# Encoder trunk: the first four weight units opened together, x loaded in four pieces and turned in a triangle

## Chip, cores and metric

One core of a Trainium2 chip. The metric is device microseconds of one execution; the kernel before takes 1910.95 us, the median of 3 runs (1910.9 to 1911.2).

## What is computed

A two-layer encoder trunk in float32 on 512 tokens (two sequences of 256) of width 1024, with shared weights. Both layers are a feed-forward half step, a mixer and a second feed-forward half step, each behind an RMS norm:

```python
def rmsnorm(x, g):
    y = xf * lax.rsqrt(jnp.mean(xf * xf, axis=-1, keepdims=True) + EPS)
    return (y * g.astype(jnp.float32)).astype(x.dtype)

def swiglu(x, wg, wu, wd):
    return (jax.nn.silu(x @ wg) * (x @ wu)) @ wd

for layer in range(DEPTH):
    x = x + 0.5 * swiglu(rmsnorm(x, norm_g[layer, 0]), ...)
    x = x + mix            # pooling and Hyena convolution, then neighbourhood attention
    x = x + 0.5 * swiglu(rmsnorm(x, norm_g[layer, 2]), ...)
```

The feed-forward width is 2816. The change touches only the start: the load of x and the first columns of the first feed-forward.

## The kernel before

Activations lie transposed: eight chunks of 128 channels by 512 tokens. A **unit** is 128 output columns of a weight matrix, 8 (or 11) tiles of 128x128. SyncE loads it (512 KB) into one of four buffers raw0 to raw3 (L255), ScalarE makes the high part wh (L288), VectorE the low part wl (L295), and TensorE multiplies three times for each chunk k, wh by xh, wh by xl and wl by xh (L832, L835, L836, one **triple**). There are two buffers wh and two wl, used by turns. A unit of 8 chunks is 24 products into one PSUM bank.

The phase `up0` takes 11 rounds of four units (gate, up, gate, up; j = 0 to 3). Units are counted through: round 0 has units 0 to 3, round 1 has units 4 to 7. VectorE scales each bank by the norm factor rbc (L610), ScalarE takes Silu of the gate (L349), VectorE multiplies (L620) and splits into hh (L353, ScalarE) and hl (L622). The split of unit u is written into each engine's program behind the end of unit u-2 (`ahead`, `split_high`), and SyncE loads unit u when the low split of unit u-3 is done.

The norm's factor is not needed by the products, since it is applied behind them. ScalarE squares each chunk (L337), GpSimd sums them (L1152), TensorE takes the mean by a product with a constant matrix (`norm_mean`, L885), ScalarE takes the root (L341), and VectorE the reciprocal (`norm_factor`, L597).

The opening before the change: ScalarE's queue issues the constants `cst` (the identity among them) and the parameter rows `vrow`; SyncE's queue loads x in four transfers and then weights. TensorE turns vrow (L889), then all of x in 32 transposes into the eight banks (L897). VectorE copies each bank to x (L662), ScalarE makes xh (L335) and its square (L337), VectorE xl (L584). Two weight units are split among these. TensorE goes through unit 0 chunk by chunk, waiting for each xl. Behind its eighth square ScalarE issues seven transfers that lay out a bias table in memory (L397, `bias_by_column<-in_rpb`), which the attention reads much later. In `first` the mean stands behind the first triple of unit 1, and reciprocal and scaling run beside units 1 and 2.

Each engine works its own program in order. A semaphore wait holds all that stands behind it on that engine.

## Time and profile before

| | |
|---|---|
| median of 3 runs | 1910.95 us |
| span of the profiled execution | 1909.3 us |
| around the span (median less span) | 1.65 us |
| TensorE busy | 1887.2 us, 99% |
| VectorE busy | 921.8 us, 48% |
| ScalarE busy | 647.1 us, 34% |
| GpSimd busy | 79.7 us, 4% |

The profiled execution's own time is not listed apart from its span; 1.65 us is what lies between the span and the median of the runs. Busy time of TensorE counts pipelined products, so its share says that it hardly pauses and not that it is at its peak. Names of the form ACTq are a queue's DMA issues, which the engine's busy time does not contain.

### The profile page before, as it was taken

How to read it: one execution, taken by the hardware profiler on the slowest of the kernel's cores; microseconds unless marked ns; L12 is line 12 of the kernel's file. 1: busy time of each engine (PE TensorE's matmuls, PEld its weight loads, DVE VectorE, ACT ScalarE, POOL GpSimd, SP SyncE). 2: the span in 40 equal slices, each digit the busy share in tenths (PEclk: the TensorE clock that was granted, in tenths of full speed). 3: DMA queues.
4: the chain of work that ended last, by engine and by line, in shares of the span. 5: the costliest groups of instructions: out<-in, count | busy, mean ns of one | idle time of the engine just before them, and what ended most of it. 6: DMA issues, size and time to landing. Idle time of an engine off the chain costs nothing.

```text
span 1909.3 us, 23383 instructions
## 1 busy us (share of the span) xinstructions
PE 1887.2 (99%) x8579; PEld 1537.3 (81%) x8579; DVE 921.8 (48%) x1166; ACT 647.1 (34%) x859; POOL 79.7 (4%) x63
## 2 busy tenths in 40 slices
PE   6999999999999999999999999999999999999999
PEld 5888888878688888888888888888777788888887
DVE  6444444366555444433544443336776654444321
ACT  4333332233243333322333232225656533333221
POOL 2000000012300000000000000001111000000000
PEclk9999999999999999999999999999999999999999
DMA  6333333243033333333233334323222133333331
GB/s 174 92 98 99 99 105 101 81 133 92 30 91 97 99 97 91 113 97 97 78 99 99 97 91 120 91 83 94 64 82 83 55 100 93 94 99 103 112 107 52
DMA packets 349165, 180.34 MB, mean 94 GB/s; under 512 B 12922, under 2 KB 347525, under 8 KB 349126
## 3 DMA queue, kind: packets, MB, share of 16 engines
q1 hardware_dynamic: 333504, 169.89, 30.6%
q10 hardware_dynamic: 15622, 9.93, 2.0%
q8 instruction: 24, 0.39, 0.1%
q14 instruction: 15, 0.12, 0.0%
HBM read 177.70 MB, written 3.93 MB: 95 GB/s over the span
## 4 chain that ended last, share of the span: by engine, by line
PE 98%; DVE 1%; DMA 0%; ACT 0%; issue 0%; ACTq 0%
PE bank L832 31%; PE bank L836 30%; PE bank L835 30%; PE bank L957 1%; PE bank L1138 1%; PE bank L1122 1%; PE bank L970 1%; PE bank L948 1%; DVE xl L584 0%; DMA vrow<-in_v_params 0%; PE bank L978 0%; PE bank L1110 0%; PE bank L937 0%; PE bank L885 0%; PE bank L1088 0%; PE bank L922 0%
## 5 line engine op out<-in xcount | busy, mean ns | idle before, releaser
L295 DVE TENSOR_TENSOR wl<-raw,wh 128x1024 fp32r<-128x1024 f32 (+1 forms) x296 | 393.4, 1329 | 685.5 <-ACT wh L288 684.1
L832 PE MATMUL bank<-xh,wh 128*128 128x512 f32 x1728 | 682.6, 395 | 6.7 <-DVE xl L584 6.7
L835 PE MATMUL bank<-xl,wh 128*128 128x512 f32 x1728 | 674.0, 390 | 0.0
L836 PE MATMUL bank<-xh,wl 128*128 128x512 f32 x1728 | 673.5, 390 | 0.0
L288 ACT ACTIVATE wh<-raw 128x1024 fp32r<-128x1024 f32 (+1 forms) x296 | 333.7, 1127 | 515.4 <-PE bank L836 515.0
L832 PEld LDWEIGHTS bank<-xh,wh 128*128 128x128 f32 x1728 | 324.8, 188 | 85.9 <-issue 12.9
L836 PEld LDWEIGHTS bank<-xh,wl 128*128 128x128 f32 x1728 | 325.0, 188 | 68.6
L835 PEld LDWEIGHTS bank<-xl,wh 128*128 128x128 f32 x1728 | 325.1, 188 | 66.4 <-issue 1.4
L832 PE MATMUL bank<-hh,wh 128*128 128x512 f32 x704 | 274.9, 391 | 0.0
L836 PE MATMUL bank<-hh,wl 128*128 128x512 f32 x704 | 274.0, 389 | 0.0
L835 PE MATMUL bank<-hl,wh 128*128 128x512 f32 x704 | 273.9, 389 | 0.0
L832 PEld LDWEIGHTS bank<-hh,wh 128*128 128x128 f32 x704 | 132.2, 188 | 28.1 <-issue 1.2
L836 PEld LDWEIGHTS bank<-hh,wl 128*128 128x128 f32 x704 | 132.2, 188 | 27.6
L835 PEld LDWEIGHTS bank<-hl,wh 128*128 128x128 f32 x704 | 132.2, 188 | 27.3
L353 ACT ACTIVATE hh<-ua 128x512 f32 (+1 forms) x88 | 55.6, 632 | 247.3 <-DVE ua L620 247.3
L349 ACT ACTIVATE ga<-ga 128x512 f32<-128x512 f32 x88 | 55.7, 632 | 165.9 <-DVE ga L610 165.9
L622 DVE TENSOR_TENSOR hl<-ua,hh 128x512 f32 (+1 forms) x88 | 61.0, 693 | 79.2 <-ACT hh L353 79.2
L335 ACT ACTIVATE xh<-x,vec 128x512 fp32r<-128x512 f32 (+1 forms) x48 | 34.7, 723 | 132.4 <-DVE x L655 125.2
L610 DVE TENSOR_TENSOR ga<-bank,rbc 128x512 f32<-128x512 f32 x100 | 68.4, 684 | 8.9 <-PE bank L836 8.8
L610 DVE TENSOR_TENSOR ua<-bank,rbc 128x512 f32<-128x512 f32 x88 | 60.2, 684 | 12.1 <-PE bank L836 12.1
L620 DVE TENSOR_TENSOR ua<-ga,ua 128x512 f32<-128x512 f32 x88 | 60.9, 692 | 5.8 <-DVE ua L610 0.5
L584 DVE SCALAR_TENSOR_TENSOR xl<-x,vec,xh 128x512 fp32r<-128x512 f32 (+1 forms) x48 | 40.6, 856 | 37.1 <-ACT xh L335 37.1
(144 smaller groups left out, 1023.4 us busy)
## 6 DMA issues: line engine op xcount, KB each, us to landing
raw<-in_ffn_w_gate SPq DMA_DIRECT2D x88, 512.0 KB, 3.8
raw<-in_ffn_w_up SPq DMA_DIRECT2D x88, 512.0 KB, 3.9
raw<-in_ffn_w_down SPq DMA_DIRECT2D x64, 704.0 KB, 4.5
raw<-in_w_qkv SPq DMA_DIRECT2D x24, 512.0 KB, 3.8
raw<-in_w_in_ab SPq DMA_DIRECT2D x16, 512.0 KB, 3.9
raw<-in_w_out_ab SPq DMA_DIRECT2D x8, 512.0 KB, 3.6
raw<-in_w_o SPq DMA_DIRECT2D x8, 512.0 KB, 3.6
braw<-bias_by_column ACTq DMA_DIRECT2D x16, 192.0 KB, 3.8
```

The costliest lines, as they stand in the source:

```text
L288: act.activation(wh[w][:, 0:ph.kt, :], raw[r][:, 0:ph.kt, :], ACT.Copy).then_inc(high, 1)
L295: dve.tensor_tensor(wl[w][:, 0:ph.kt, :], raw[r][:, 0:ph.kt, :], wh[w][:, 0:ph.kt, :].bitcast(F32), ALU.subtract).then_inc(low, 1)
L335: act.activation(xh[:, bass.ds(d, 1), :], x[:, bass.ds(d, 1), :], ACT.Copy, scale=col(V_NORM + norm * KD + d)).then_inc(xh_done, 1)
L349: act.activation(g[:, :], g[:, :], ACT.Silu).then_inc(silu_done, 1)
L353: act.activation(hh[:, bass.ds(f, 1), :], u[:, :], ACT.Copy).then_inc(hh_done, 1)
L584: dve.scalar_tensor_tensor(out=xl[:, bass.ds(d, 1), :], in0=x[:, bass.ds(d, 1), :], scalar=col(V_NORM + norm * KD + d), in1=xh[:, bass.ds( ...
L610: dve.tensor_tensor(out, src, r, ALU.mult).then_inc(evac, 1)
L620: dve.tensor_tensor(u[:, :], g[:, :], u[:, :], ALU.mult).then_inc(h_done, 1)
L622: dve.tensor_tensor(hl[:, bass.ds(f, 1), :], u[:, :], hh[:, bass.ds(f, 1), :].bitcast(F32), ALU.subtract).then_inc(hl_done, 1)
L832: pe.matmul(out, wh[w][:, k, :], hi[:, at, :], start=start, stop=False)
L835: pe.matmul(out, wh[w][:, k, :], lo[:, at, :], start=False, stop=False)
L836: return pe.matmul(out, wl[w][:, k, :], hi[:, at, :], start=False, stop=stop)
```

## The change

x comes in four pieces of 256 channels. Each is two transfers, and behind each stands one of the first four weight loads, without a wait. The constants' identity part is loaded by itself, ahead of vrow, and the rest behind it (`ident_in`, `const_in`). Units 2 and 3 get wh and wl buffers of their own (`wh_c`, `wh_d`, `wl_c`, `wl_d`), which lie where hh will be written later. x is turned two chunks at a time into banks 4 to 7; ScalarE takes xh and VectorE xl from PSUM, VectorE then copies to x. After each pair of chunks one weight unit is split. The products go through chunks and units in a triangle (`opening`). Round 0 of `up0` is taken out of the general loops of all engines and written out, and the seven bias transfers follow at its end on ScalarE.

```diff
--- before.py
+++ after.py
@@ -153,3 +153,4 @@
         hh, hl = region([("hh", [P, KF, TOK], F32R), ("hl", [P, KF, TOK], F32R)])
-        (xrow,) = region([("xrow", [P, TT, D])])
+        xrow, wh_c, wl_c, wh_d, wl_d = region([("xrow", [P, TT, D]), ("wh_c", [P, KD, P], F32R), ("wl_c", [P, KD, P], F32R),
+                                               ("wh_d", [P, KD, P], F32R), ("wl_d", [P, KD, P], F32R)])
         own = ExitStack()
@@ -183,3 +184,3 @@
             ("rqk", [P, 2, TT, 2]), ("kwide", [P, TT, P])])
-        wh, wl = wh + [wh2], wl + [wl2]
+        wh, wl = wh + [wh2, wh_c, wh_d], wl + [wl2, wl_c, wl_d]
@@ -189,2 +190,3 @@
         raw_in = [sem(f"raw_in{s}") for s in range(4)]
+        ident_in = sem("ident_in")
         const_in, vec_in, filt_in, out_in = sem("const_in"), sem("vec_in"), sem("filt_in"), sem("out_in")
@@ -245,8 +247,2 @@
         def _(sp):
-            for n in range(4):
-                half = slice(n // 2 * (D // 2), (n // 2 + 1) * (D // 2))
-                sp.dma_start(xrow[:, n % 2 * 2:n % 2 * 2 + 2, half],
-                             (a["x_sample"] if n % 2 else a["x_prompt"])[0].rearrange("(t p) c -> p t c", p=P)[:, :, half])\
-                  .then_inc(x_in[n], 16)
             def load(ph, i):
@@ -256,4 +252,14 @@
+            for n in range(4):
+                cols = slice(n * 2 * P, (n + 1) * 2 * P)
+                for s, src in enumerate((a["x_prompt"], a["x_sample"])):
+                    sp.dma_start(xrow[:, 2 * s:2 * s + 2, cols], src[0].rearrange("(t p) c -> p t c", p=P)[:, :, cols])\
+                      .then_inc(x_in[n], 16)
+                sp.dma_start(raw[n][:, 0:KD, :], unit_source(phases[0], 0, n)).then_inc(raw_in[n], 16)
             for ph in phases:
-                if ph.name == "w_in":
+                if ph.name == "up0":
+                    with sp.Fori(1, ph.iters) as i:
+                        load(ph, i)
+                elif ph.name == "w_in":
                     for i in range(ph.iters):
@@ -269,3 +275,9 @@
+        def opens(ph, i):
+            return ph.name == "up0" and isinstance(i, int) and i == 0
         def split_place(ph, i, j):
+            if opens(ph, i) and j > 1:
+                return j + 1, j
             return (j if ph.name == "qkv" or early(ph, i, j) else j % 2), j
@@ -285,4 +297,5 @@
             act.wait_ge(raw_in[r], 16 * (ph.uses0[r] + 1 + i))
-            back = 2 if early(ph, i, j) else 1
-            act.wait_ge(unit_done, ph.unit(i, j) - back + UNIT_CREDIT)
+            if not opens(ph, i):
+                back = 3 if ph.name == "up0" and isinstance(i, int) and i == 1 else 2 if early(ph, i, j) else 1
+                act.wait_ge(unit_done, ph.unit(i, j) - back + UNIT_CREDIT)
             act.activation(wh[w][:, 0:ph.kt, :], raw[r][:, 0:ph.kt, :], ACT.Copy).then_inc(high, 1)
@@ -305,3 +318,5 @@
-            if after_first or ph.name in NORM_OF or ph.name == "w_o":
+            if ph.name == "up0":
+                first = 1
+            elif after_first or ph.name in NORM_OF or ph.name == "w_o":
                 body(0, False)
@@ -320,4 +335,5 @@
-            act.dma_start(cst[:, :], a["c_small"]).then_inc(const_in, 16)
+            act.dma_start(ident, a["c_small"][:, C_ID:C_ID + P]).then_inc(ident_in, 16)
             act.dma_start(vrow[:, :], a["v_params"]).then_inc(vec_in, 16)
+            act.dma_start(cst[:, P:C_ALL], a["c_small"][:, P:C_ALL]).then_inc(const_in, 16)
             act.dma_start(zT[:, :], a["c_z"]).then_inc(filt_in, 16)
@@ -383,11 +399,21 @@
+            act.wait_ge(vec_done, 1)
             for d in range(KD):
-                act.wait_ge(evac, d + 1 + EVAC_CREDIT)
-                if d >= 2:
-                    act.wait_ge(acc_done, d - 1)
-                residual_parts(0, d, d % 2)
-                if d == 1:
-                    split_high(act, phases[0], 0, 0)
-                if d == 4:
-                    split_high(act, phases[0], 0, 1)
+                act.wait_ge(x_mm, d + 1)
+                act.activation(xh[:, d, :], bank[4 + d % 4][:, :], ACT.Copy, scale=col(V_NORM + d)).then_inc(xh_done, 1)
+                if d % 2:
+                    split_high(act, phases[0], 0, d // 2)
+                    for e in (d - 1, d):
+                        act.wait_ge(evac, e + 1 + EVAC_CREDIT)
+                        if e >= 2:
+                            act.wait_ge(acc_done, e - 1)
+                        act.activation(sqtmp[:, e % 2, :], x[:, e, :], ACT.Square).then_inc(sq_done, 1)
+            split_high(act, phases[0], 1, 0)
+            act.wait_ge(const_in, 16)
+            norm_std(0)
+            evacuate(phases[0], 0, 0)
+            split_high(act, phases[0], 1, 1)
+            evacuate(phases[0], 0, 1)
+            evacuate(phases[0], 0, 2)
+            evacuate(phases[0], 0, 3)
@@ -555,3 +581,3 @@
             dve.wait_ge(vec_mm, 1)
-            dve.tensor_copy(vec[:, :], bank[7][:, 0:V_ALL]).then_inc(vec_done, 1)
+            dve.tensor_copy(vec[:, :], bank[0][:, 0:V_ALL]).then_inc(vec_done, 1)
             dve.wait_ge(vec_done, 1)
@@ -659,10 +685,11 @@
-            for d in range(KD):
-                dve.wait_ge(x_mm, d + 1)
-                dve.tensor_copy(x[:, d, :], bank[d][:, :]).then_inc(evac, 1)
-            split_low(dve, phases[0], 0, 0)
-            for d in range(KD):
-                part_low(0, d)
-                if d == 4:
-                    split_low(dve, phases[0], 0, 1)
+            for d in range(0, KD, 2):
+                for e in (d, d + 1):
+                    dve.wait_ge(xh_done, e + 1)
+                    dve.scalar_tensor_tensor(out=xl[:, e, :], in0=bank[4 + e % 4][:, :], scalar=col(V_NORM + e),
+                                             in1=xh[:, e, :].bitcast(F32), op0=ALU.mult, op1=ALU.subtract)\
+                       .then_inc(xl_done, 1)
+                for e in (d, d + 1):
+                    dve.tensor_copy(x[:, e, :], bank[4 + e % 4][:, :]).then_inc(evac, 1)
+                split_low(dve, phases[0], 0, d // 2)
@@ -759,2 +786,11 @@
+            norm_factor(0)
+            evacuate(phases[0], 0, 0)
+            split_low(dve, phases[0], 1, 0)
+            evacuate(phases[0], 0, 1)
+            sums_cleared(0)
+            split_low(dve, phases[0], 1, 1)
+            evacuate(phases[0], 0, 2)
+            evacuate(phases[0], 0, 3)
             for ph in phases:
@@ -886,14 +922,48 @@
-            pe.wait_ge(const_in, 16)
-            pe.wait_ge(vec_in, 16)
-            pe.transpose(bank[7][:, 0:V_ALL], vrow[:, :], cst[0:V_ALL, C_ID:C_ID + V_ALL]).then_inc(vec_mm, 1)
-            for d in range(KD):
-                if d % 4 == 0:
-                    pe.wait_ge(x_in[d // 4 * 2], 16)
-                    pe.wait_ge(x_in[d // 4 * 2 + 1], 16)
-                if d == 7:
-                    pe.wait_ge(vec_done, 1)
-                for t in range(TT):
-                    last = pe.transpose(bank[d][:, t * P:(t + 1) * P], xrow[:, t, d * P:(d + 1) * P], ident)
-                last.then_inc(x_mm, 1)
+            def opening():
+                ph = phases[0]
+                pe.wait_ge(ident_in, 16)
+                pe.wait_ge(vec_in, 16)
+                pe.transpose(bank[0][:, 0:V_ALL], vrow[:, :], cst[0:V_ALL, C_ID:C_ID + V_ALL]).then_inc(vec_mm, 1)
+                def turn_x(n):
+                    pe.wait_ge(x_in[n], 32)
+                    for d in (2 * n, 2 * n + 1):
+                        if d >= 4:
+                            pe.wait_ge(evac, d - 3 + EVAC_CREDIT)
+                        for t in range(TT):
+                            last = pe.transpose(bank[4 + d % 4][:, t * P:(t + 1) * P], xrow[:, t, d * P:(d + 1) * P], ident)
+                        last.then_inc(x_mm, 1)
+                def tiles(j, ks):
+                    w = split_place(ph, 0, j)[0]
+                    for k in ks:
+                        if k == 0:
+                            pe.wait_ge(low, ph.unit(0, j) + 1 + LOW_CREDIT)
+                        pe.wait_ge(xl_done, k + 1)
+                        after = bank_read(ph, 1, 0) if j == 3 and k == KD - 1 else None
+                        last = three(bank[j][:, :], w, k, j, xh, xl, k, start=k == 0, stop=k == KD - 1, between=after)
+                        if k == KD - 1:
+                            last.then_inc(unit_done, 1)
+                turn_x(0)
+                pe.wait_ge(vec_done, 1)
+                tiles(0, range(0, 2))
+                turn_x(1)
+                tiles(0, range(2, 4))
+                tiles(1, range(0, 4))
+                turn_x(2)
+                for j in range(2):
+                    tiles(j, range(4, 6))
+                turn_x(3)
+                tiles(2, range(0, 6))
+                for j in range(3):
+                    tiles(j, range(6, 8))
+                tiles(3, range(0, 4))
+                pe.wait_ge(const_in, 16)
+                norm_mean(0)
+                tiles(3, range(4, 8))
+            opening()
@@ -1096,3 +1166,4 @@
-                first()
+                if name != "up0":
+                    first()
                 with pe.Fori(1, ph.iters) as i:
```

The order listings below show each engine's instructions as built, with the waits of each. Names are those of the code, a number behind a name is its buffer.

**TensorE, from the start of the program.** Before:

```order
L889 MATMUL bank<-cst,vrow 128x106 [waits vec_in,const_in]
L897 MATMUL bank<-cst,xrow 128x128 [waits x_in1,x_in0]
L897 MATMUL bank<-cst,xrow 128x128 x15
L897 MATMUL bank<-cst,xrow 128x128 [waits x_in3,x_in2]
L897 MATMUL bank<-cst,xrow 128x128 x11
L897 MATMUL bank<-cst,xrow 128x128 [waits vec_done]
L897 MATMUL bank<-cst,xrow 128x128 x3
L832 MATMUL bank<-xh,wh 128x512 [waits xl_done,evac,low]
L835 MATMUL bank<-xl,wh 128x512
```

Now:

```order
L928 MATMUL bank0<-cst,vrow 128x106 [waits vec_in,ident_in]
L936 MATMUL bank4<-cst,xrow 128x128 [waits x_in0]
L936 MATMUL bank4<-cst,xrow 128x128 x3
L936 MATMUL bank5<-cst,xrow 128x128 x4
L868 MATMUL bank0<-xh,wh0 128x512 [waits xl_done,low,vec_done]
L871 MATMUL bank0<-xl,wh0 128x512
L872 MATMUL bank0<-xh,wl0 128x512
L868 MATMUL bank0<-xh,wh0 128x512 [waits xl_done]
L871 MATMUL bank0<-xl,wh0 128x512
L872 MATMUL bank0<-xh,wl0 128x512
L936 MATMUL bank6<-cst,xrow 128x128 [waits x_in1]
L936 MATMUL bank6<-cst,xrow 128x128 x3
```

All 32 transposes stood ahead of the first product; now the third and fourth chunk are turned behind six products, and those wait for xl, for the first low split (`low`) and for vec. The mean (before behind the first triple of unit 1) now stands behind the fourth triple of unit 3.

**ScalarE, from the last square of the opening on.** Before:

```order
L337 ACTIVATE sqtmp<-x 128x512
L397 DMA bias_by_column<-in_rpb 16x64x64 x7
L288 ACTIVATE wh0<-raw2 128x1024 [waits unit_done,raw_in2]
L341 ACT_TABLE_LOAD
L341 ACTIVATE rbc<-bank7,cst 128x512 [waits mean_mm]
L288 ACTIVATE wh1<-raw3 128x1024 [waits unit_done,raw_in3]
L349 ACT_TABLE_LOAD
L349 ACTIVATE ga0<-ga0 128x512 [waits evac]
L353 ACTIVATE hh<-ua0 128x512 [waits low,h_done]
```

Now (from the split of unit 4, which follows the last square):

```order
L301 ACTIVATE wh0<-raw0 128x1024 [waits unit_done,raw_in0]
L357 ACT_TABLE_LOAD [waits mean_mm]
L357 ACTIVATE rbc<-bank7,cst 128x512 [waits const_in]
L365 ACT_TABLE_LOAD
L365 ACTIVATE ga0<-ga0 128x512 [waits evac]
L301 ACTIVATE wh1<-raw1 128x1024 [waits unit_done,raw_in1]
L369 ACTIVATE hh<-ua0 128x512 [waits low,h_done]
L365 ACTIVATE ga1<-ga1 128x512 [waits evac]
L369 ACTIVATE hh<-ua1 128x512 [waits low,h_done]
L423 DMA bias_by_column<-in_rpb 16x64x64 x7
L327 UNCONDITIONAL_BRANCH
L327 ISA
```

The seven bias issues stood ahead of the split of unit 2 (`wh0<-raw2`, its L288); now they stand behind the second hh of round 0 and ahead of the loop, whose first split is that of unit 6. The load of the root's table now carries the wait for the mean (`mean_mm`), where before only the root itself did.

**VectorE, from the last xl of the opening on.** Before:

```order
L584 SCALAR_TENSOR_TENSOR xl<-x,vec,xh 128x512 [waits xh_done] x3
L295 TENSOR_TENSOR wl0<-raw2,wh0 128x1024 [waits high]
L597 RECIPROCAL rbc<-rbc 128x512 [waits std_done]
L295 TENSOR_TENSOR wl1<-raw3,wh1 128x1024 [waits high,rbc_done]
L610 TENSOR_TENSOR ga0<-bank0,rbc 128x512 [waits unit_done]
L610 TENSOR_TENSOR ua0<-bank1,rbc 128x512 [waits unit_done]
L620 TENSOR_TENSOR ua0<-ga0,ua0 128x512 [waits evac,silu_done]
L622 TENSOR_TENSOR hl<-ua0,hh 128x512 [waits hh_done]
```

Now (from the low split of unit 3 on):

```order
L308 TENSOR_TENSOR wl_d<-raw3,wh_d 128x1024 [waits high]
L623 RECIPROCAL rbc<-rbc 128x512 [waits std_done]
L636 TENSOR_TENSOR ga0<-bank0,rbc 128x512 [waits unit_done,rbc_done]
L308 TENSOR_TENSOR wl0<-raw0,wh0 128x1024 [waits high]
L636 TENSOR_TENSOR ua0<-bank1,rbc 128x512 [waits unit_done]
L646 TENSOR_TENSOR ua0<-ga0,ua0 128x512 [waits evac,silu_done]
L648 TENSOR_TENSOR hl<-ua0,hh 128x512 [waits hh_done]
```

The reciprocal stood ahead of the low split of unit 3; now it stands behind that, and ahead of the scaling of bank 0 and of the low split of unit 4.

## Rows read from the trace of the kernel before

**Rows 1.** The page: busy us (share of the span) and instructions of each engine

```profile
PE 1887.2 (99%) x8579; PEld 1537.3 (81%) x8579; DVE 921.8 (48%) x1166; ACT 647.1 (34%) x859; POOL 79.7 (4%) x63
```

**Rows 2.** Who waited for whom, TensorE: us in total, times, longest

```profile
PE bank L832 <- DVE xl L584: 6.7, 3, 5.5
```

**Rows 3.** Chain that ended last, its first pieces: start us, us, what

```profile
1.24 7.66 DMA vrow<-in_v_params
9.45 2.58 PE bank L897 x12
12.05 3.68 DVE x L662 x6
...
17.95 8.42 DVE xl L584 x5
```

**Rows 4.** Timeline of the opening: start us, us, engine, line, out<-in, [idle before <-releaser]

```profile
3.85 1.28 ACT L335 ACT_TABLE_LOAD   x1 [3.85 <-issue]
...
9.24 5.00 PE L897 MATMUL bank<-cst,xrow 128*128 128x128 f32 x32
...
10.34 0.69 DVE L662 COPY x<-bank 128x512 f32<-128x512 f32 x1 [0.32 <-PE bank L897]
...
19.78 0.77 PE L832 MATMUL bank<-xh,wh 128*128 128x512 f32 x1 [5.53 <-DVE xl L584]
...
20.34 0.63 PE L835 MATMUL bank<-xl,wh 128*128 128x512 f32 x1
...
20.77 0.63 PE L836 MATMUL bank<-xh,wl 128*128 128x512 f32 x1
```

**Rows 5.** One stretch of PE: length, busy (x), granted clock, DMA share, GB/s

```profile
18.80:25.60 6.80, 5.75 (x11) 0.50 0.50 127
```

**Rows 6.** Timeline, TensorE: first products of units 4 and 6

```profile
47.64 0.39 PE L832 MATMUL bank<-xh,wh 128*128 128x512 f32 x1
...
58.52 0.39 PE L832 MATMUL bank<-xh,wh 128*128 128x512 f32 x1
```

**Rows 7.** Single lines, every instruction: duration ns min/median/max, first and last start

```profile
L818 DVE SCALAR_TENSOR_TENSOR al<-bank,vec,ah x4: 751/751/752, 503.9 to 506.5; 128x512 fp32r<-128x512 f32 x4
...
L534 ACT ACTIVATE ah<-bank,vec x4: 687/687/687, 503.2 to 505.8; 128x512 fp32r<-128x512 f32 x4
...
L295 DVE TENSOR_TENSOR wl<-raw,wh x8: 1214/1225/2306, 15.6 to 59.8; 128x1024 fp32r<-128x1024 f32 x8
...
L1152 POOL TENSOR_TENSOR sqacc<-sqacc,sqtmp x8: 1268/1538/2067, 12.5 to 24.3; 128x512 f32<-128x512 f32 x8
```

**Rows 8.** DMA issues up to 60 us: KB each, median us from issue to landing

```profile
cst<-in_c_small ACTq DMA_DIRECT2D x1, 98.5 KB, 4.4
```

**Rows 9.** Timeline from the mean to the reciprocal, 31 to 37 us

```profile
31.09 1.02 PE L885 MATMUL bank<-sqacc,mean_of 128*128 128x512 f32 x2
...
31.74 1.28 ACT L341 ACT_TABLE_LOAD   x1
...
33.04 0.69 ACT L341 ACTIVATE rbc<-bank,cst 128x512 f32<-128x512 f32 x1
...
33.76 3.35 DVE L597 RECIPROCAL rbc<-rbc 128x512 f32<-128x512 f32 x1 [0.78 <-ACT rbc L341]
```

**Rows 10.** Timeline, ScalarE and its DMA issues from 22 us

```profile
22.59 0.69 ACTq L397 DMA_DIRECT2D bias_by_column<-in_rpb  x1
23.18 0.61 ACT L337 ACTIVATE sqtmp<-x 128x512 f32<-128x512 f32 x1
23.31 7.22 ACTq L397 DMA_DIRECT2D bias_by_column<-in_rpb  x6
30.67 1.06 ACT L288 ACTIVATE wh<-raw 128x1024 fp32r<-128x1024 f32 x1 [6.88 <-PE bank L836]
```

**Rows 11.** Timeline, VectorE, round 0, from its second scaling to the next low split

```profile
39.92 0.68 DVE L610 TENSOR_TENSOR ua<-bank,rbc 128x512 f32<-128x512 f32 x1
...
43.62 1.22 DVE L295 TENSOR_TENSOR wl<-raw,wh 128x1024 fp32r<-128x1024 f32 x1 [0.28 <-ACT wh L288]
```

## The prediction

> **What bounds the kernel now.** Start with the page. TensorE is busy for 99% of the span [rows 1], so what stops or slows it counts in full, and other engines count only where TensorE waits for them. The view of who waited for whom shows where that is: three waits of its products for xl add up to 6.7 us, and all three are in the opening [rows 2]. The chain that ended last starts with the landing of vrow, the transposes, the copies of x and xl [rows 3]. The timeline shows the first product at 19.78 us after a pause of 5.5 us [rows 4]. The products then wait for xl chunk by chunk, at a granted clock of 0.50 from 18.8 to 25.6 us, which is 1.2 GHz [rows 5]. Behind the eighth chunk the opening holds no further wait. The mark I use is the first product of unit 6, at 58.52 us; that of unit 4 is at 47.64 [rows 6]. Behind unit 6 the program is the old one, so its delay is the kernel's.
>
> **Durations.** One triple, warm: (58.52 - 47.64)/16 = 0.68 us. At half clock two products start at 20.34 and 20.77 [rows 4], 0.43 us apart, so a triple takes 1.29. Twelve transposes take 2.58 us at first [rows 3], so eight take 1.7; the other 20 of 32 end at 14.24 [rows 4], 0.11 each, so eight warm ones take 0.9. xh from PSUM: 0.69 by the nearest form; xl from PSUM: 0.75 by the nearest form; a low split 1.23 [rows 7]. A copy of a bank is 0.68 to 0.69 [rows 4].
>
> **The opening.** vrow landed at 8.90 [rows 3]. Ahead of it the ScalarE queue now carries less, and x comes in shorter runs between which it can pass. No row shows by how much. The bounds are 8.9 (no gain) and 5.2, where the load ahead of it landed before (4.4 behind its issue at 0.75 [rows 8]); I take 8.0, nearer to the row of vrow itself. The first chunk was turned 1.44 us behind that landing, by the start of its copy [rows 4]: now 9.45. ScalarE's table load stood at 3.85 without a wait [rows 4]. In the new program it carries the wait for the first chunk, so its 1.28 us join the chain: 10.8. Then xh of two chunks to 12.15, xl of two to 12.95, two copies to 14.3, the low split of unit 0 to 15.55. The first product starts at 15.6, 4.2 us earlier than before.
>
> Then the triangle turns into a relay, because TensorE is one queue. Two triples at half clock to 18.2 and two chunks turned to 19.9; only then can ScalarE start on those. The third chunk's xl is ready at 20.6. Unit 1 needs wl1, which stands on VectorE behind two xl and two copies: 24.0. Four triples, two of them at half clock if it rises at 25.7 as before, to 28.0; two chunks turned to 28.9; another pause of 1.1 for xl; four triples to 32.7, two chunks to 33.6. From here nothing is late: 16 triples to 44.5, the mean 0.9 (its two passes show 1.02, the last part of it under the next product [rows 9]), four triples to 48.1. Before, this point was at 47.64. **Start gained 4.2 us, end lost 0.5**: late xl was swapped for late transposes.
>
> The loads are in time. The old order had all of x, 2 MB, landed by the 16th of the 32 transposes, about 12 us. At that rate the second piece of x (1.5 MB into the queue) lands by 9 us and is needed at 18.2, unit 1's weights by 12 and are needed near 20, the third piece (2.6 MB) by 16 and is needed at 28, and the last of all 4 MB by 24, needed behind 33. Copies of x cost nothing of their own: they stand behind xl, and where wl1 waits for them they are in the 24.0. Squares end beside the copies.
>
> **Shared ports.** Beside GpSimd's sums, which start from 12.5 to 24.3, a low split took 2.31 us, where it takes 1.23 alone [rows 7], and five xl took 8.42, 1.7 each [rows 3]. xl now reads a bank. If it slows down in the same way, two rounds lose some 2 us each; but six copies of banks took 3.68 beside the sums [rows 3], 0.61 apart and not slowed, so I take none. The low splits keep two SBUF operands and start at about the moment when the squares end, for wl0 and wl1 within 0.1 us of GpSimd's start: 0 to 1.1 us each; I take 0.3 each, 0.6. The Trainium skill (SBUF — State Buffer, "SBUF: two separate sides") says that only a DVE operation with two SBUF inputs, or in a two-port mode, locks against GpSimd; by that the xl are free and the splits are not, and the sum would be as I have it.
>
> **The norm comes late (first stall).** The mean stood behind the first triple of unit 1, with 23 triples to hide its tail. Now it stands four triples ahead of the end of round 0. On its heels: the root's table load 1.28, since it now carries the wait for the mean, root 0.69, reciprocal 3.35 [rows 9], then on VectorE the scaling of bank 0 (0.68) and only behind it the low split of unit 4 (1.23). That is 7.2, with four hand-overs 7.4. From 45.5 this gives 52.9. TensorE ends its four triples at 48.1, so it stands for 4.8 us, and unit 4 starts at 52.9, 5.3 later than at 47.64.
>
> **The bias transfers come late (second stall).** ScalarE issues seven, from 22.59 to 30.53: 7.9 us, because the queue fills and holds it; the split behind starts at 30.67 [rows 10]. There this cost nothing, since the split was released by unit 0's last product, by the same row. Now they stand behind the second hh of round 0 and ahead of the split of unit 6. From wl4 at 52.9 VectorE goes through scaling, product, hl, clearing and wl5, which took from 39.92 to 44.84 with 0.28 idle [rows 11], 4.6 us, and then two scalings and a product at 0.69: 2.1. The second hh can go out at 59.6, and the transfers behind it. They hold ScalarE to 67.5; high split 1.06 [rows 10], low split 1.23: unit 6 can start at 69.8. TensorE ends units 4 and 5 at 52.9 + 10.9 = 63.8 and stands for 6.0 us. **Unit 6 is at 69.8 against 58.52: 11.3 late.** Unit 7's splits (ready near 74) are in time, and from there the old rhythm holds.
>
> **The clock.** Before, a pause of 5.5 us was followed by 6.8 us at 0.50, of which 5.8 lay behind the first product [rows 4, 5]. A product at half clock loses half its time. Behind the second stall that is 0 to 3.4 us; I take 2.0. Behind the first stall a slow spell only fills the second one.
>
> **Sum:** 11.3 + 0.6 + 2.0 = 13.9 us. The profiled execution's span is 1909.3 and 1.65 lies around it, which makes the median of 1910.95; 1909.3 + 13.9 + 1.65 = 1924.9 us, 0.7% slower. A measurement of this kernel tells about 0.2%, 3.8 us, from no change.
>
> **Rivals.**
>
> *The issues hold ScalarE less.* The first took 0.69, the seven 7.9 [rows 10]. Seven at 0.69 are 4.8: the second stall is 2.9, and a pause as short may leave the clock alone. 13.9 - 3.1 - 2.0 = 8.8, 1919.7. For it: the queue is empty when they start. Against it: it was empty at 22.59 too. 15%.
>
> *The opening runs at the full clock,* since TensorE's pauses are shorter than the 5.5 us of before. Four triples and eight transposes gain 0.6 and 0.1 each: 3.2 less, partly lost again to VectorE's chain; I take 2.3: 1922.6. The first two of those triples still follow a pause of over 5 us, which speaks against it. 12%.
>
> *A table load costs more than its row.* The row shows 1.28 and the root 0.02 behind it, where the load had time in hand [rows 9]. If a load on the chain brings as much again, both loads on it add 2.6: 1927.5. The row does not show it. The Trainium skill (ScalarE: Activation LUTs, "What ACT_TABLE_LOAD costs") says that a switch of tables costs about 1.38 us of drain beside the load. 8%.
>
> *Faster: ScalarE's queue runs ahead.* The first bias issue starts at 22.59, ahead of a square at 23.18 that precedes it in the program [rows 10]. If issues and loads never hold compute behind them, the second stall and both table loads leave the chain: unit 6 at 52.9 - 2.6 + 10.9 = 61.2, 2.7 late. It decides from where the opening gains those 2.7: with vrow at 5.2 (2.8) and the early clock (2.3) it would be 2.4 early, 1908.5. With less of either it ends within 0.2%. Against it: running ahead helps what stands in front, and the split behind the issues did start only when they were over. 4% for faster; 7% more for ending within 0.2%, the same with a weaker opening.
>
> **How the numbers follow.** The forecast with its own bounds, 1921 to 1929 (the clock 0 to 3.4, wl0 and wl1 0 to 2.2, vrow -2.8 to +0.9), has 54%. The range of 1916 to 1930 adds the short issues, the full clock and most of the table loads' case; faster, same and the far ends are left out. Faster 0.04, same 0.07, slower 0.89.
>
> **What would show it.** The first product near 15.6, unit 4 near 53, unit 6 near 70 to 72. TensorE's waits: a new one of about 5 us in front of unit 4, put down to VectorE's low split or scaling behind the reciprocal, and one of about 6 in front of unit 6. ScalarE's seven issues from near 59.5 to 67, the split of unit 6 right behind. The granted clock at 0.50 for some us behind 64. The root's table load starting behind the mean. Wrong it is if the split of unit 6 starts before the issues end, if the reciprocal starts before unit 3's last triples, or if units 4 to 7 run without a gap.

## Result and profile after

| | before | changed |
|---|---|---|
| median of the runs made side by side, us | 1911.1 (1910.9 to 1912.5, 4 runs) | 1922.8 (1921.6 to 1923.6, 4 runs) |
| span of the profiled execution, us | 1909.3 | 1921.8 |
| first product, us | 19.78 | 14.26 |
| product of the mean, us | 31.09 | 42.73 |
| unit 4 / unit 5 / unit 6, first product, us | 47.64 / 53.08 / 58.52 | 51.11 / 58.06 / 67.73 |
| from unit 6 to the end of the span, us | 1850.8 | 1854.1 |

**0.6% slower**: the ratio is 1.006, with a 95% interval of 1.0046 to 1.0074. The forecast was 1924.9 with a range of 1916 to 1930. The change starts multiplying 5.5 us earlier and reaches unit 6 9.2 us later, and 3.3 us more are lost behind unit 6. The two add up to the 12.5 us between the spans. Of the experiments' runs one, of "low split first", took 2576.2 us at a mean granted clock of 0.694 and is left out of its row below.

The page of the changed kernel, busy us of each engine, beside [rows 1]. TensorE is busy for 5.6 us more with the same 8579 instructions, so it ran slower somewhere.

```profile
PE 1892.8 (98%) x8579; PEld 1540.6 (80%) x8579; DVE 915.6 (48%) x1166; ACT 647.1 (34%) x859; POOL 81.3 (4%) x63
```

Who waited for whom, TensorE, changed kernel: us in total, times, longest. This answers to [rows 2].

```profile
PE bank L868 <- DVE wl L308: 9.8, 4, 5.1
PE bank L928 <- DMA vrow<-in_v_params: 7.1, 1, 7.1
PE bank L871 <- DVE ga L636: 3.9, 1, 3.9
PE bank L1027 <- ACT pt L454: 2.0, 1, 2.0
PE bank L868 <- DVE xl L689: 1.8, 2, 1.1
```

The 6.7 us for xl have become 1.8. In their place stand 9.8 for low splits and 3.9 for the scaling of bank 0 (ga). Of the 9.8, 5.1 stand ahead of the first product and are no loss: they replace the 5.5 of [rows 4]. In front of unit 6 stand 4.07, in front of unit 4 0.40 (timeline below). The remaining 0.25 stands in front of unit 1.

The chain that ended last, changed kernel, its first pieces, beside [rows 3]: start us, us, what.

```profile
1.24 5.68 DMA vrow<-in_v_params
...
8.40 1.28 ACT L403
...
9.70 0.69 ACT xh L403
...
10.42 1.41 DVE xl L689 x2
...
13.02 1.14 DVE wl L308
...
14.26 0.76 PE bank L868
15.02 0.43 PE bank L871
...
17.15 1.72 PE bank L936 x8
...
18.90 0.70 ACT xh L403
...
19.62 0.75 DVE xl L689
...
21.57 1.14 DVE wl L308
...
22.75 0.76 PE bank L868
23.51 0.24 PE bank L871
```

The table load (L403, 1.28) is on the chain, with xh right behind it. Then the relay: TensorE's first six products end at 17.15 and it turns two chunks by 18.87. ScalarE, which waited 4.36 us for them, starts on the first of the two at 18.04 and on the second at 18.90; unit 1 starts at 22.75. Products are 0.43 apart until then and 0.24 or less behind 23.5. The granted clock in the records is 1.00 over this whole stretch. The 0.43 is the spacing that the kernel before shows where its records say 0.50 [rows 4, 5], so I take it for half speed; no record here confirms it.

Timeline of the changed kernel from the mean to unit 6, beside [rows 6, 9, 10]: start us, us, engine, line, out<-in, [idle before <-releaser].

```profile
42.73 1.02 PE L921 MATMUL bank<-sqacc,mean_of 128*128 128x512 f32 x2
...
43.83 1.28 ACT L357 ACT_TABLE_LOAD   x1 [5.22 <-PE bank L921]
...
45.12 0.69 ACT L357 ACTIVATE rbc<-bank,cst 128x512 f32<-128x512 f32 x1
...
45.84 3.35 DVE L623 RECIPROCAL rbc<-rbc 128x512 f32<-128x512 f32 x1 [9.82 <-ACT rbc L357]
49.23 0.69 DVE L636 TENSOR_TENSOR ga<-bank,rbc 128x512 f32<-128x512 f32 x1
49.84 1.22 DVE L308 TENSOR_TENSOR wl<-raw,wh 128x1024 fp32r<-128x1024 f32 x1
...
49.98 0.50 PE L871 MATMUL bank<-xl,wh_d 128*128 128x512 f32 x1 [3.92 <-DVE ga L636]
...
51.11 0.80 PE L868 MATMUL bank<-xh,wh 128*128 128x512 f32 x1 [0.40 <-DVE wl L308]
...
57.67 0.63 ACT L369 ACTIVATE hh<-ua 128x512 fp32r<-128x512 f32 x1 [0.76 <-DVE ua L646]
57.68 7.05 ACTq L423 DMA_DIRECT2D bias_by_column<-in_rpb  x7
...
65.36 1.06 ACT L301 ACTIVATE wh<-raw 128x1024 fp32r<-128x1024 f32 x1 [7.05 <-issue]
66.45 1.22 DVE L308 TENSOR_TENSOR wl<-raw,wh 128x1024 fp32r<-128x1024 f32 x1 [7.42 <-ACT wh L301]
...
67.73 0.80 PE L868 MATMUL bank<-xh,wh 128*128 128x512 f32 x1 [4.07 <-DVE wl L308]
```

Both stalls are there as forecast. Between the mean and the scaling of bank 0 TensorE has four triples, and the tail takes 6.5 us. Later it stands for 4.07 us because the split of unit 6 begins when the seven bias issues are over.

Stretches of TensorE in the changed kernel, beside [rows 5]: length, busy (x), granted clock, DMA share, GB/s.

```profile
50.60:54.10 3.50, 3.10 (x8) 0.51 0.48 141
67.70:71.10 3.40, 3.37 (x8) 0.50 0.54 155
1511.50:1515.00 3.50, 3.50 (x12) 0.51 0.00 1
```

Each stall is followed by 3.4 us at 1.2 GHz. The third stretch lies in the attention, late in the program, which the change does not touch: there TensorE stands for 2.0 us for pt in both kernels (the wait of L1027 above). The kernel before shows the same wait, and in its profiled execution no stretch at half clock follows:

```profile
PE bank L957 <- ACT pt L428: 2.0, 1, 2.0
...
1500.20:1503.70 3.50, 3.43 (x21) 1.00 0.00 0
```

Both stretches begin within 0.4 us of the product that ends this wait. In 3.50 us TensorE starts 21 products before and 12 in the changed kernel.

### The profile page after: what moved, and what is told of

Its sections match the earlier page's. It is cut to its first block, busy times and chain, and to the rows that moved or that the text cites. A ratio compares the mean times of both kernels' runs of the same rounds, so it can differ in the third digit from the quotient of the medians.

```text
span 1921.8 us, 23377 instructions
## 1 busy us (share of the span) xinstructions
PE 1892.8 (98%) x8579; PEld 1540.6 (80%) x8579; DVE 915.6 (48%) x1166; ACT 647.1 (34%) x859; POOL 81.3 (4%) x63
## 4 chain that ended last, share of the span: by engine, by line
PE 97%; DVE 1%; ACT 1%; ACTq 0%; DMA 0%; issue 0%; DVEq 0%
PE bank L868 30%; PE bank L871 30%; PE bank L872 30%; PE bank L1027 1%; PE bank L1209 1%; PE bank L1193 1%; PE bank L1040 1%; PE bank L1018 1%; PE bank L1048 0%; PE bank L1181 0%; ACTq L423 0%; PE bank L1007 0%; DVE wl L308 0%; DMA vrow<-in_v_params 0%; PE bank L921 0%; PE bank L936 0%
## 5 line engine op out<-in xcount | busy, mean ns | idle before, releaser
L308 DVE TENSOR_TENSOR wl<-raw,wh 128x1024 fp32r<-128x1024 f32 (+1 forms) x294 | 389.8, 1326 | 683.3 <-ACT wh L301 681.8
L351 ACT ACTIVATE xh<-x,vec 128x512 fp32r<-128x512 f32 (+1 forms) x40 | 29.0, 724 | 125.2 <-DVE x L681 125.2
L1264 POOL TENSOR_TENSOR bmask<-braw,cst 128x768 f32<-128x768 f32 x8 | 12.4, 1552 | 907.2 <-DMA braw<-bias_by_column 781.8
```

Of the source, the lines that this page charges most:

```text
L308: dve.tensor_tensor(wl[w][:, 0:ph.kt, :], raw[r][:, 0:ph.kt, :], wh[w][:, 0:ph.kt, :].bitcast(F32), ALU.subtract).then_inc(low, 1)
L351: act.activation(xh[:, bass.ds(d, 1), :], x[:, bass.ds(d, 1), :], ACT.Copy, scale=col(V_NORM + norm * KD + d)).then_inc(xh_done, 1)
```

## The experiments

Two numbers of each run separate causes: where the marks lie, and what passes between unit 6 and the end of the span. Marks are first products in us; "halves" lists where the granted clock was 0.50 (3.4 us long each, unless a length stands beside it), without the last 3 us of the span.

| kernel | median us (lowest to highest, runs) | ratio to before, 95% | first | mean | unit 4 | unit 6 | rest | halves |
|---|---|---|---|---|---|---|---|---|
| before | 1911.2 (12 runs) | | 19.78 | 31.09 | 47.64 | 58.52 | 1850.8 | 18.8 (6.8) |
| changed | 1922.8 (1921.6 to 1923.6, 4) | 1.0046 to 1.0074 | 14.26 | 42.73 | 51.11 | 67.73 | 1854.1 | 50.7, 67.7, 1511.6 |
| bias issues early | 1916.1 (1914.7 to 1917.5, 8) | 1.0015 to 1.0037 | 13.41 | 41.58 | 49.96 | 62.22 | 1850.7 | 49.2 |
| mean early | 1920.7 (1920.0 to 1921.1, 4) | 1.0031 to 1.0065 | 13.71 | 39.16 | 47.53 | 64.35 | 1855.0 | 62.9 (6.8), 1510.2 |
| low split first | 1921.8 (1919.6 to 1922.7, 4) | 1.0035 to 1.0067 | 14.39 | 42.58 | 50.85 | 67.03 | 1853.9 | 49.8, 66.8, 1510.7 |
| one wait | 1920.5 (1919.3 to 1922.2, 4) | 1.0029 to 1.0063 | 13.10 | 41.77 | 48.81 | 65.61 | 1854.7 | 63.7 (6.8), 1510.9 |
| all four | 1909.1 (1907.8 to 1910.0, 11) | 0.9976 to 0.9994 | 12.43 | 37.68 | 44.16 | 55.08 | 1852.2 | 1497.6 |
| before, bias issues late | 1917.9 (1917.3 to 1918.2, 6) | 1.0019 to 1.0043 | 19.68 | 31.02 | 47.53 | 62.16 | 1853.9 | 18.1 (6.8), 62.5, 1506.3 |
| one turn ahead | 1905.3 (1904.8 to 1906.2, 5) | 0.9951 to 0.9979 | 12.57 | 33.80 | 40.28 | 51.19 | 1852.3 | 1493.8 |
| two turns ahead | 1902.1 (1901.9 to 1903.6, 5) | 0.9936 to 0.9963 | 12.49 | 32.09 | 38.58 | 49.48 | 1850.8 | none |

Each ratio is against runs of the kernel before on the same chip. Their median was 1911.2 (12 runs) beside the first four variants, 1912.3 (17 runs) beside "all four" and "before, bias issues late", and 1912.4 (9 runs) beside the last two; these runs fall into two groups (last section), so the medians differ by which group holds more. The marks, the rest and the halves are those of one profiled execution of each kernel.

The column "rest" adds up. Without a stretch at half clock behind unit 6 it is 1850.7 to 1850.8. One stretch of 3.4 us in the attention makes it 1852.2 to 1852.3, so it costs 1.4 to 1.6, about 1.5. One more behind unit 6 makes it 1853.9 to 1854.1 and costs 1.6 to 1.9 (it is 1854.7 to 1855.0 where that one is 6.8 long). The two kinds of stretch account for the whole column, so all else is in the marks. Up to 1.0 us of the marks is no effect of an edit. The loads of vrow and of the identity are the same in the changed kernel and in all its variants, yet vrow took 4.84 us ("bias issues early") to 5.82 ("low split first") to land, and 5.68 in the changed kernel. The first product follows it (13.41, 14.39 and 14.26).

### Bias issues early

```diff
+            def bias_rows(rs):
+                for r in rs:
...
                         act.activation(sqtmp[:, e % 2, :], x[:, e, :], ACT.Square).then_inc(sq_done, 1)
+                if d == 3:
+                    bias_rows(range(0, 4))
+                if d == 7:
+                    bias_rows(range(4, DR))
             split_high(act, phases[0], 1, 0)
...
-            for r in range(DR):
...
```

The body of bias_rows is that of the loop removed: one issue for each r.

> The changed kernel with one edit: four of the seven bias transfers are issued behind the fourth square of the opening (near 22 us, where ScalarE waits 4.3 us), three behind the eighth (near 35.6), none behind round 0. My theory (the issues hold ScalarE and so unit 6): ScalarE splits unit 6 as soon as unit 4 is done, the 4.1 us wait in front of unit 6 and the half clock behind it (1.7 us) go; unit 6 starts at 51.1 + 10.9 + 1.5 = 63.5 instead of 67.7, the time is 1922.8 - 5.8 = 1917.0, to within the 1.6 us of a half-clock stretch near 1510 us. Rival (the wait in front of unit 6 is VectorE's, whose work comes late behind the reciprocal): unit 6 stays within 1 us of 67.7 and the time within 1 us of 1922.8.

Measured: 1916.1, against 1917.0 expected. Unit 6 stands 5.4 us behind unit 5 (56.78), with no stall: the second one is gone, and its half-clock stretch with it. This profiled execution has none in the attention either, which the expectation left open. The issues still cost their time, elsewhere. In the opening they hold ScalarE's queue while it waits for TensorE anyway:

```profile
20.76 4.05 ACTq L404 DMA_DIRECT2D bias_by_column<-in_rpb  x4
...
25.41 1.26 ACT L410 ACTIVATE xh<-bank,vec 128x512 fp32r<-128x512 f32 x2 [4.02 <-PE bank L941]
```

(Timeline; the xh of the next chunks starts at 25.41 behind a wait for TensorE's transposes, not for the queue.) Against the changed kernel unit 6 is 5.5 us earlier, of which 0.85 is the first product; the rest is 3.4 shorter for want of the two stretches. This makes the 8.9 us between the spans.

### Mean early

```diff
-                tiles(3, range(0, 4))
                 pe.wait_ge(const_in, 16)
                 norm_mean(0)
-                tiles(3, range(4, 8))
+                tiles(3, range(0, 8))
```

> The changed kernel with the mean in front of unit 3's first triple instead of behind its fourth. My theory (the tail mean, table load, root, reciprocal, scaling, low split sets unit 4): the mean starts at 40.0 instead of 42.7, everything behind it on ScalarE and VectorE moves up by 2.7; unit 4 starts at 48.4 instead of 51.1 and unit 6, whose chain hangs on the same tail, at 65.0 instead of 67.7; time 1920.1, or 1.7 less where the first pause no longer brings the half clock. Rival (unit 4 waits for its weights or for the sums): unit 4 stays at 51.

Measured: 1920.7. The wait for ga shrinks from 3.92 to 1.20, by the 2.7 of four triples (4 x 0.68); unit 4 comes 3.6 earlier, of which 0.55 is the first product and 0.3 lies in the rest of the opening. Behind so short a wait no stretch at half clock follows, so units 4 and 5 run at full speed and reach the second stall sooner: it is 5.6 us here (TensorE's longest wait) instead of 4.07. The stretch at half clock there is 6.8 us long instead of 3.4, from 62.9.

### Low split first

```diff
+            split_low(dve, phases[0], 1, 0)
             norm_factor(0)
             evacuate(phases[0], 0, 0)
-            split_low(dve, phases[0], 1, 0)
             evacuate(phases[0], 0, 1)
```

> The changed kernel with the low split of unit 4 in front of the reciprocal on VectorE, as it stood before the change in front of unit 2's turn. VectorE is idle from 36.0 to 45.8, so the split costs nothing there. My theory: unit 4 waits only for the scaling of bank 0 and starts at 50.6 at the latest (0.5 earlier, the two last products of unit 3 still stand behind the scaling), the chain to unit 6 shortens by 1.2; unit 6 at 66.5, time 1921.6. Rival (the 3.9 us wait in front of unit 3's last products hides the split): the same for unit 4, and unit 6 stays at 67.7.

Measured: 1921.8, not told apart from the changed kernel's 1922.8. The low split hides beside the mean, yet unit 4 gains 0.26 only and unit 6 0.70. TensorE's last triple waits for ga in its second product, so the 3.92 us stay whole. Moving the split saves the 0.40 behind them, but half clock begins 0.9 us earlier here (49.8) and stretches the two products in between, which leaves 0.11; the other 0.15 of unit 4's gain lies in the opening. The chain to unit 6 is shorter by the 1.2 expected: the second hh starts at 56.45 instead of 57.67. The seven issues behind it then take 7.57 us instead of 7.05, and 0.5 of the gain is lost in them.

### One wait

ScalarE no longer waits for vec_done and const_in; TensorE waits for vec_done before the last transpose of the first chunk instead, and has waited for const_in before the mean.

```diff
-            act.wait_ge(vec_done, 1)
             for d in range(KD):
...
-            act.wait_ge(const_in, 16)
             norm_std(0)
...
+                            if d == 0 and t == TT - 1:
+                                pe.wait_ge(vec_done, 1)
                             last = pe.transpose(bank[4 + d % 4][:, t * P:(t + 1) * P], xrow[:, t, d * P:(d + 1) * P], ident)
```

> The changed kernel with one wait each in front of ScalarE's first xh and of the root: TensorE waits for vec and for the constants instead, ahead of what ScalarE waits for anyway. Both table loads then carry no wait, as in the kernel before. My theory: the first table load runs before the first chunk is turned, the first product comes at 13.0 instead of 14.26; the root's load runs before the mean, the reciprocal is 1.28 earlier against the mean; unit 4 at 51.1 - 1.3 (tail) - up to 1.3 (opening, less what the clock's rise gives back) = 48.6 to 49.8, unit 6 at 65.2 to 66.4, time 1920.3 to 1921.5. The rival that a load costs twice its row: twice that, unit 4 at 46 to 48, time near 1918.

Measured: 1920.5. Timeline of this kernel:

```profile
8.39 0.69 ACT L402 ACTIVATE xh<-bank,vec 128x512 fp32r<-128x512 f32 x1 [2.65 <-PE bank L936]
...
41.77 1.02 PE L919 MATMUL bank<-sqacc,mean_of 128*128 128x512 f32 x2
...
42.83 0.69 ACT L357 ACTIVATE rbc<-bank,cst 128x512 f32<-128x512 f32 x1 [3.88 <-PE bank L919]
```

xh and the root now follow TensorE without a table load between. From the mean's start to the root's it is 1.06 us here and 2.39 in the changed kernel: 1.33 saved, one load of 1.28. So a load costs its row on this chain and no more. The Trainium skill (ScalarE: Activation LUTs, "What ACT_TABLE_LOAD costs") speaks of some 1.38 us of drain beside it; in the changed kernel the load starts at 43.83, lasts 1.28, and the root starts at 45.12. No drain behind it shows on this chain.

### All four

> The changed kernel with all four edits together: bias issues spread over the opening, the mean in front of unit 3, unit 4's low split in front of the reciprocal, one wait at each table load. My theory: the mean ends near 39.7 to 41, root without a table load 0.7, reciprocal 3.35, scaling 0.7, so bank 0 is free at 44.5 to 46.5 and TensorE, at 44.4 to 45.7 on the last triple of unit 3, waits 1 us at most; unit 4 at 45.5 to 47.6, unit 6 at 56.4 to 58.5, no half clock there. Against the kernel before (unit 4 at 47.64, unit 6 at 58.52) 0 to 2 us faster: 1909 to 1911. The rival that the triangle itself costs time: unit 6 at 60 or later and a time of 1913 or more even without the two waits.

Measured: 1909.1, as expected; the ratio of 0.9976 to 0.9994 is a small gain, and it lies below 1 throughout. TensorE no longer waits for the first ga, and unit 6 is at 55.08, 3.4 earlier than before. The loss of the change thus lies in these four places: without them the time is 13.7 us less than that of the changed kernel, of which 0.7 is vrow's earlier landing (4.99 against 5.68). The gain over before stays small, since the relay is left. Who waited for whom from 9 to 36 us in this kernel:

```profile
DVE xl L692 <- ACT xh L409: 11.2, 4, 4.6
ACT xh L409 <- PE bank L941: 9.5, 4, 4.3
```

VectorE waits for ScalarE's xh, and that for TensorE's transposes, while TensorE multiplies what it has.

### Before, with the bias issues late

The kernel before, with one edit: the seven issues are put behind the first pass, as in the changed kernel.

> The kernel before the change with one edit: the seven bias transfers stand behind the second hh of round 0, where the change put them, instead of behind the eighth square. All else is the old opening. My theory: they are issued from 51.6 to about 59.2, ScalarE splits unit 6 at 59.3 instead of 53.3, the low split ends at 61.6, unit 6 starts at 61.6 instead of 58.52: 3.1 us lost, 1914.2, and up to 1.7 more if the pause brings half clock. Rival (ScalarE's queue runs ahead of its DMA issues): no change, 1911.

Measured: 1917.9, 3.7 above the expected 1914.2. Waits of TensorE in this kernel:

```profile
PE bank L834 <- DVE wl L295: 3.6, 1, 3.6
```

Its timeline:

```profile
51.54 0.63 ACT L353 ACTIVATE hh<-ua 128x512 fp32r<-128x512 f32 x1 [2.69 <-DVE ua L622]
51.54 7.62 ACTq L471 DMA_DIRECT2D bias_by_column<-in_rpb  x7
...
59.80 1.06 ACT L288 ACTIVATE wh<-raw 128x1024 fp32r<-128x1024 f32 x1 [7.62 <-issue]
...
62.16 0.52 PE L834 MATMUL bank<-xh,wh 128*128 128x512 f32 x1 [3.59 <-DVE wl L295]
```

The place of seven issues, nothing else, costs the kernel before 6.8 us of span (1916.1 against 1909.3): 3.6 of stall, 1.7 at half clock behind it, and 1.5 at half clock in the attention at 1506.3, where the profile of before had none. That last 1.5 no theory had, and the 1.7 was only allowed for.

### One turn and two turns ahead

Both are "all four" with transposes given to TensorE ahead of the products that need nothing of them. In the second, two bias issues go behind the squares of chunk 5, three behind those of chunk 7 and two behind the split of unit 5. The edit to the order of TensorE in the second (the first has only the move of turn_x(1)):

```diff
                 turn_x(0)
-                tiles(0, range(0, 2))
                 turn_x(1)
+                tiles(0, range(0, 2))
+                turn_x(2)
                 tiles(0, range(2, 4))
                 tiles(1, range(0, 4))
-                turn_x(2)
+                turn_x(3)
                 for j in range(2):
                     tiles(j, range(4, 6))
-                turn_x(3)
                 tiles(2, range(0, 6))
```

> The kernel with all four edits, and the third and fourth chunk turned in front of the first two triples instead of behind them (their banks 6 and 7 are free; the second piece of x should be in by 9 us). My theory (the relay: late transposes leave ScalarE idle for 4.3 us and VectorE for 4.6 us, and unit 1's low split stands behind that): xl of the third chunk is there when TensorE gets to it, the low split of unit 1 ends at 16.5 instead of 20.7, TensorE has no pause there; unit 1 starts at 17.7 instead of 20.75, unit 6 at 52 instead of 55.1, time 1906. Rival (VectorE's and ScalarE's own work bounds the opening, not the order of the transposes): unit 1 within 0.5 us of 20.75, time 1909. Rival (x's second piece is late): the first product itself moves behind 12.4.

> As the one before, and the fifth and sixth chunk turned in front of the triples of chunks 3 and 4, the last two in front of the four triples of chunks 5 and 6; the bias issues two behind the sixth square, three behind the eighth, two behind the split of unit 5, since ScalarE's gaps near 20 us are used up. My theory: the 1.1 us pause in front of chunk 5 goes as well, unit 6 at 50.5 to 51.5, time 1904 to 1906. Rival (the sums or the reciprocal's tail, 5.8 us from the mean, bound unit 4 by then): a new wait in front of unit 3's last triple or of the mean, and no gain over turning one pair ahead.

Measured: 1905.3 and 1902.1, ratios 0.9951 to 0.9979 and 0.9936 to 0.9963. Both beat both kernels; the second is 0.5% below before and 20.7 us below the changed one, and 2 us under its expectation; unit 6 came 1.0 us earlier than expected (49.48 against 50.5), and this execution has no stretch at half clock. The first of the two waits above, from 9 to 36 us, with two turns ahead:

```profile
DVE xl L690 <- ACT xh L409: 2.7, 3, 1.2
```

From 11.2 to 2.7 us: the relay is gone. TensorE now waits nowhere for xl or the first scaling (the 0.8 for ga is a later place, and there before too), and 1.7 us for a piece of x. Waits of TensorE with two turns ahead, whole program:

```profile
PE bank L1028 <- ACT pt L455: 2.0, 1, 2.0
PE bank L939 <- DMA xrow<-in_x_sample: 1.7, 1, 1.7
PE bank L993 <- DVE ga L682: 0.8, 1, 0.8
PE bank L869 <- DVE wl L308: 0.2, 1, 0.2
```

Unit 6 is at 49.48 against 55.08 in "all four". That is 5.6 of the 7.0 us between the spans; the other 1.4 is that this execution has no stretch at half clock in the attention. The second kernel also has its bias issues in other places; what of its 1.7 us over the first (51.19 to 49.48) they bring was not measured apart.

## Why the prediction was right, step by step

The mechanism and its two places were as forecast, and the experiments show each: the early bias issues take away stall 2, the early mean cuts stall 1, and late issues alone make the kernel before slower. Sizes were off in both directions, and the two nearly cancel. The forecast added 13.9 us; the spans differ by 12.5. That the time came out this near is in part luck: the delay at unit 6 was taken 2.7 us too long, and a loss of 1.5 behind it, which no step had, made up for half of that.

- **vrow at 8.0.** It landed at 6.92. The first product came at 14.26 instead of 15.6, 1.3 less. The steps from landing to product took 7.3 us against 7.6 taken.
- **Relay, unit 1 at 24.0, mean at 44.5.** Measured 22.75 and 42.73. Of the 1.8, 1.3 is the first product; the rest is that products ran at full speed from 23.5 on, and not from the assumed 25.7.
- **First stall 4.8.** Measured 3.92 + 0.40. From the load to unit 4 it was 7.28 us against 7.4 taken, so the tail was right. The wait for bank 0's reader stands inside unit 3's last triple, behind its first product, and I had put it behind the whole triple; the two products that then follow the wait make up the other 0.5.
- **Bias issues 7.9.** From the second hh's start to the split it was 7.7 us (57.67 to 65.36), and 8.3 in the kernel before with the issues late (51.54 to 59.80). This step was right in its size. That the queue fills is the prediction's reading; the runs show how long the issues take and that the split waits for them, and none tests why.
- **Second stall 6.0.** It was 4.07. 1.5 of the difference is the stretch at half clock behind stall 1, which stretched units 4 and 5 (unit 5 stands 6.95 behind unit 4, before 5.44): as written, a slow spell there only fills the second stall. Unit 6 is at 67.73, not 69.8, and 1.8 of that comes from the opening.
- **Ports 0.6.** Nothing. The first two low splits took 1.22, though the sums ran beside them, and the wl of this row are all alike (line L308 up to 60 us: duration ns min/median/max, first and last start):

```profile
L308 DVE TENSOR_TENSOR wl<-raw,wh x4: 1216/1216/1225, 12.9 to 54.4; 128x1024 fp32r<-128x1024 f32 x4
```

- **Clock 2.0 behind stall 2.** 1.8 by the column "rest" (1854.1 less 1850.8 and 1.5).
- **What was missing:** the half-clock stretch in the attention, 1.5. No step looked behind unit 6, since the program there is the old one; that the old program may run there at another clock was not considered.

In sum: 2.7 less at unit 6 (1.8 opening, 0.6 ports, 0.2 issues, 0.1 rest) and 1.3 more behind it (0.2 less clock, 1.5 in the attention).

**Of the rivals:** *issues hold less* falls: behind round 0 the seven took 7.05 to 7.62 us in all five kernels that have them there, and 4.8 in none. *Full clock in the opening* is partly so: spacing fell to full speed at 23.5, 2.2 us before the assumed 25.7, but the first twelve products, and the transposes between them, were spaced as at half speed. More of it would have brought 0.3 and not 2.3: in "bias issues early", "mean early" and "low split first" the products were 0.23 to 0.35 apart from the second pair of chunks on, yet unit 1 stood 8.5 us behind the first product as in the changed kernel (22.75 - 14.26), since it waits for VectorE, and only behind unit 1 was 0.3 gained. *A table load costs double* falls, by "one wait" and by the row at 45.12. *ScalarE's queue runs ahead* falls: in the kernel before with the issues late, the split waited for the issues' end (7.62 <-issue), and in the changed kernel too (7.05 <-issue). An issue can start before the compute that precedes it is over (57.68 beside the hh of 57.67), but what follows the issues waits for them.

## What to carry to other kernels

When one queue both prepares (transposes) and consumes (products), issue its preparation one or two steps before the products that leave the others idle; here that took 7 us off the same program, 5.6 of them in the opening. Where transfers are issued from a compute engine's queue, count their issue time as work of that engine, and put them where it waits anyway. Before a step is moved later, count the work left to hide its tail: from the mean to unit 4's first product it was 8.4 us (42.73 to 51.11), and the triangle left four triples, 2.7.

## What the runs showed of the hardware

Seven transfers of 16x64x64 elements each hold ScalarE's queue for 7.05 to 7.62 us when issued together behind round 0, though the first of them took 0.69 [rows 10], and compute behind them starts only afterwards. Split into four and three, they took 4.05 and 2.23 ("bias issues early"), and the first two and the next three took 1.41 and 2.43 with two turns ahead: 0.7 to 0.8 each for two or three in a row, 1.0 to 1.1 each for four or seven.

A pause of TensorE of 2.0 us in the attention is followed by 3.4 us at 1.2 GHz in some executions and not in others: kernels whose program is the same from unit 6 on differ there. It costs about 1.5 us. It is the likely reason why the runs of the kernel before fall into two groups, 1910.7 to 1911.6 and 1912.2 to 1913.3, those of "bias issues early" into 1914.7 to 1915.4 and 1916.8 to 1917.5, and why four runs of two turns ahead lie within 0.2 us and the fifth 1.5 above; only the profiled executions show the stretch itself, so for the other runs this is an inference. The mean granted clock that each run lists supports it: of the 38 runs of before it is 0.998 in all 20 of the lower group and 0.997 in 14 of the 18 of the upper, and it is 0.999 and 0.997 in the groups of "bias issues early", 1.000 and 0.999 with two turns ahead. The groups of "bias issues early" lie some 2.3 us apart, more than one such stretch costs, so something more differs there. Why the stretch appears was not settled.

GpSimd, not VectorE, paid for the shared ports. The low splits kept 1.22 us beside it, and its sums went from a median of 1.54 us [rows 7] to this:

```profile
L1223 POOL TENSOR_TENSOR sqacc<-sqacc,sqtmp x8: 1276/1674/2132, 13.2 to 37.3; 128x512 f32<-128x512 f32 x8
```

The split started at 12.94 and the sums at 13.24. The Trainium skill (SBUF — State Buffer, "SBUF: two separate sides") says that whichever starts first has the pair for its whole instruction; the trace agrees here, with 1.22 us for the split and 3.46 for the first two sums. xl, which now has one operand in a bank, was not slowed beside the sums: two of them took 1.41 us beside the third pair of sums, as at 10.42, before the first.

```profile
29.98 3.57 POOL L1223 TENSOR_TENSOR sqacc<-sqacc,sqtmp 128x512 f32<-128x512 f32 x2 [4.71 <-ACT sqtmp L410]
...
32.29 1.41 DVE L689 SCALAR_TENSOR_TENSOR xl<-bank,vec,xh 128x512 fp32r<-128x512 f32 x2 [1.33 <-ACT xh L403]
```

Before the change the five xl with both operands in memory took 8.42 beside the sums [rows 3], 1.7 each.
